# Depthwise convolution of 31 taps: four groups of taps on TensorE's column tiles in place of five, fourteen taps on VectorE in place of ten

## The chip, the cores and the metric

The kernel runs on one core of one Trainium2 chip. The metric is the device time of one execution in microseconds. The kernel before takes 2666.74 us, the median of 3 runs (2666.61 to 2668.82).

## The reference, cut to what matters

The whole program is two transformer-like blocks over 512 tokens of 1024 channels (recurrent mixers, cross attention, convolutional feed-forward stages, an expert layer). The change lies in one stage of the first block, the conformer convolution, which runs once:

```python
CONV_C = 31
def causal_dwconv(x, w, b):
    K, C = w.shape
    y = lax.conv_general_dilated(
        x, w[:, None, :], window_strides=(1,), padding=[(K - 1, 0)],
        dimension_numbers=("NWC", "WIO", "NWC"), feature_group_count=C)
    return y + b

def conformer_conv(x, norm, w1, b1, dw_w, dw_b, ln_g, ln_b, w2, b2):
    h = rms_norm(x, norm) @ w1 + b1
    h = jax.nn.glu(h, axis=-1)
    h = causal_dwconv(h, dw_w, dw_b)
    h = jax.nn.silu(layer_norm(h, ln_g, ln_b))
    return h @ w2 + b2
```

Each of the 1024 channels is convolved over time with 31 taps of its own: tap k multiplies the signal 30-k steps back.

## The kernel before, in words

Activations lie channel-major, 128 channels by 512 tokens to a tile, so the stage has 8 channel tiles, j = 0 to 7. Weights of the large products come in a stream of units of 1 MB; ScalarE rounds each (`w_hi`, L549), VectorE takes what is left (`w_lo`, L553), and a product is three matmuls, hi by hi, hi by lo, lo by hi (`split_matmul`, L566 through the helper). Three slots hold such units.

There is no scheduler. Every engine has its own program, in the order in which its function is written, and engines meet at semaphores. For the stage these are:

- **TensorE** (`pe_conformer`, L1516): first the pointwise products of tile 0; then for each j the pointwise products of tile j+1 (two banks, c1 and c2, 48 matmuls), the convolution part of tile j, and a matmul with ones over tile j-1 for the layer norm's mean. For j = 7 two key products of the next stage (`pe_keys`, of `xa_m_hi`) stand where the pointwise products would.
- **VectorE** (`dve_conformer`, L1596): for each j the gated unit `glu` into `c_t1`, then the taps one after the other, each a multiply-add of a shifted `c_t1` into `c_h` (L1649, recorded at the helper's L588), with the weights of a later tile (`c_w`, L1609) and the sum of TensorE's part of tile j-1 (`sums`, L1617) in between; then `pointwise(j+1)`: the split of a weight unit, and the two copies t2 (L1633) and t1 (L1635) out of the banks, scaled.
- **ScalarE** (`act_conformer`, L1558): the sigmoid of the gate (L1570), and tap 30 with the bias, which opens `c_h` (L1573); then the rounding of a unit. For j = 7 a rounding stands ahead of the sigmoid.
- **SyncE** (`sp_conformer`, L1499): when glu(j) is done, 16 DMAs (L1510) build four stacks of 128 partitions: 32 channels, four times over, each copy one time step later. The stacks of even j are `c_stack`; those of odd j lie in `square`, `root` and `c_mu`.

TensorE's part of the convolution: with a stack as the moving operand, one matmul with a 128 by 32 weight adds up four taps of 32 channels. Four such matmuls, one for each 32 columns of the array and 32 partitions of the bank, make a group of four taps for all 128 channels. `C_GROUPS` says how many groups there are:

```python
            for m in range(C_GROUPS):
                first = C_BASE + 4 * m
                for g in range(4):
                    mm = matmul(T, b[g * QUARTER:(g + 1) * QUARTER, first:], c_w[:, i, g * C_GROUPS + m, :],
                                c_stacks[i][g][:, 0:S - first], m == 0, m == C_GROUPS - 1)
```

and VectorE has what is left of the first 30 taps:

```python
            for k in range(CONV_C - 1 - 4 * C_GROUPS):
                s = CONV_C - 1 - k
                V.wait_ge(*dve_c.now())
                stt(V, c_h[:, j, s:], c_t1[:, i, 0:S - s], c_tap(j)(k), c_h[:, j, s:], ALU.mult, ALU.add).then_inc(
                    *dve_c.mark("tap", j, k))
```

All instructions of the stage that the steps below speak of are fp32, and each fp32 matmul has two records in the profile, so a group of four is eight records.

Of the kernel before, what the change touches and what calls it, by code (L numbers as in the profile page):

```python
# [44 lines left out]
NO_ROW = 1 << 16  # L45
LEVELS = 6
QUARTER = 32
C_GROUPS = 5

# [118 lines left out]
def _conv_taps(w):  # L170
    p = np.arange(P)
    rows = np.zeros((P, KT, 4, C_GROUPS), np.float32)
    for k in range(4):
        for m in range(C_GROUPS):
            by_tile = w[CONV_C - 2 - 4 * m - k].reshape(KT, 4, QUARTER)
# [62 lines left out]
def build(nc, stream, vectors, consts, rconsts, x_in, mem_in, gates_w, group_w, lora_w,  # L238
# [13 lines left out]
    def sb(ctx, name, shape, dt=F32):  # L252

        one = ctx.enter_context(nc.sbuf_tensor(name, shape, dt))
        over = math.prod(shape[1:]) * (1 if dt == U8 else 4) % 64
        if 0 < over <= 32:
            ctx.enter_context(nc.sbuf_tensor(f"fill{next(fill)}", [P, 8], F32))
        return one
# [65 lines left out]
    with ExitStack() as ph:  # L324
        with ExitStack() as conv:
# [3 lines left out]
            c_stack = sb(conv, "c_stack", [P, 4, S])  # L329
            c_w = sb(conv, "c_w", [P, 2, 4 * C_GROUPS, QUARTER])  # L330
            c_rows = sb(conv, "c_rows", [P, 4 * C_GROUPS * KT + QUARTER])
        with ExitStack() as inner:
# [232 lines left out]
    def matmul(T, out_ap, lhsT, rhs, first=True, last=True):  # L565
        return T.matmul(out_ap, lhsT, rhs, start=first, stop=last, skip_group_check=True)  # L566
# [949 lines left out]
    def pe_conformer(T):  # L1516
# [13 lines left out]
        for j in range(KT):  # L1530
# [7 lines left out]
            T.wait_ge(*c_stacked[j % 2].at(j, 3, 3))  # L1538
# [5 lines that stand above are left out]
# [2040 lines left out]
```

## Time and profile before

| what | value |
|---|---|
| median of 3 runs | 2666.74 us |
| profiled execution, its own time | 2666.76 us |
| its span | 2665.5 us |
| TensorE busy | 2484.3 us, 93% |
| VectorE busy | 1429.4 us, 54% |
| ScalarE busy | 925.1 us, 35% |
| granted TensorE clock, mean | 0.97 |
| the conformer's eight tiles | about 812 to 947 us of the span |

The busy shares are averages over the whole program. The change touches one stage of some 135 us, so the views of that stage are the ones to read: which engine waits there, and for whom. A row of the timeline gives start, duration, engine, line, what is written and read, the count, and in brackets the idle time before it with what ended it.

### The profile page before, as it was taken

The numbers are of one execution on the slowest core, as the hardware profiler recorded it, in microseconds if no ns is written. First come the engines' busy times: TensorE is split into PE (matmuls) and PEld (weight loads), VectorE is DVE, ScalarE is ACT, GpSimd is POOL, SyncE is SP. The second block draws the span as 40 slices with busy tenths as digits, with TensorE's granted clock in tenths as the row PEclk, the third lists the DMA queues.
The fourth block names the chain that finished last, engine by engine and source line by source line (L and its number), as shares of the span: only waits on it lengthen the run. The fifth ranks groups of instructions, "written<-read, shape, count | busy, mean of one in ns | idle before, by whom it ended". The sixth has DMA issues, their size and how long they took to land. (4 is left out here: it accounts for less than half of the span.)

```text
span 2665.5 us, 42794 instructions
## 1 busy us (share of the span) xinstructions
PE 2484.3 (93%) x18420; PEld 1867.3 (70%) x18420; DVE 1429.4 (54%) x1943; ACT 925.1 (35%) x1248; POOL 220.5 (8%) x190
## 2 busy tenths in 40 slices
PE   8989999999999989999999999998887778879997
PEld 6767877888876657878888878877666667733332
DVE  6776446454557764455454667556665746421112
ACT  4454233232333243243232344244453433411111
POOL 1002010000010000010000020001101100133331
PEclk9999999999999999999999999999898889989998
DMA  4223322322234422222222235342021134489994
GB/s 177 85 75 119 111 76 84 109 93 97 95 100 129 127 90 81 94 95 95 95 95 95 95 111 191 114 174 77 4 53 25 21 107 138 153 339 375 398 381 179
DMA packets 100570, 343.29 MB, mean 129 GB/s; under 512 B 41376, under 2 KB 49952, under 8 KB 66592
## 3 DMA queue, kind: packets, MB, share of 16 engines
q1 hardware_dynamic: 86560, 332.13, 35.4%
q0 software_dynamic: 13824, 8.44, 1.0%
q8 instruction: 147, 2.41, 0.4%
q14 instruction: 39, 0.32, 0.0%
HBM read 368.29 MB, written 30.93 MB: 150 GB/s over the span
## 5 line engine op out<-in xcount | busy, mean ns | idle before, releaser
L566 PE MATMUL bank<-xg_hi,w_hi 128*128 128x512 f32 x1504 | 597.9, 398 | 12.1 <-DVE xg_lo L588 12.1
L566 PE MATMUL bank<-xg_lo,w_hi 128*128 128x512 f32 x1504 | 586.8, 390 | 0.0
L566 PE MATMUL bank<-xg_hi,w_lo 128*128 128x512 f32 x1504 | 586.7, 390 | 0.0
L553 DVE TENSOR_TENSOR w_lo<-w_raw,w_hi 128x2048 fp32r<-128x2048 f32 x165 | 378.7, 2296 | 193.1 <-ACT w_hi L549 192.9
L549 ACT ACTIVATE w_hi<-w_raw 128x2048 fp32r<-128x2048 f32 x165 | 314.3, 1905 | 248.1 <-PE bank L566 217.8
L566 PEld LDWEIGHTS bank<-xg_hi,w_hi 128*128 128x128 f32 x1504 | 283.1, 188 | 78.4 <-DVE w_lo L553 12.3
L566 PEld LDWEIGHTS bank<-xg_lo,w_hi 128*128 128x128 f32 x1504 | 283.0, 188 | 63.9 <-issue 6.0
L566 PEld LDWEIGHTS bank<-xg_hi,w_lo 128*128 128x128 f32 x1504 | 282.9, 188 | 59.4
L566 PE MATMUL bank<-f_h_hi,w_hi 128*128 128x512 f32 x384 | 151.4, 394 | 0.0
L566 PE MATMUL bank<-f_h_hi,w_lo 128*128 128x512 f32 x384 | 150.6, 392 | 0.0
L566 PE MATMUL bank<-f_h_lo,w_hi 128*128 128x512 f32 x384 | 149.1, 388 | 0.0
L566 PE MATMUL bank<-e_over_ring,e_h_turned 128*64 128x512 f32 x560 | 124.4, 595 | 0.0
L734 DVE TENSOR_TENSOR x<-bank,x 128x512 f32<-128x512 f32 x80 | 55.0, 687 | 122.9 <-PE bank L566 122.9
L3296 DVE TENSOR_TENSOR e_he<-e_he,bank 128x256 f32<-128x256 f32 x24 | 10.1, 421 | 171.0 <-ACT e_he L3117 171.0
L588 DVE SCALAR_TENSOR_TENSOR f_g<-f_z,vec_sb,f_g 128x510 f32<-128x510 f32 x96 | 72.0, 750 | 44.2 <-ACT f_g L1445 42.5
L1445 ACT ACTIVATE f_g<-f_z,vec_sb 128x512 f32<-128x512 f32 x48 | 39.2, 816 | 150.5 <-DVE f_z L1470 150.5
L566 PEld LDWEIGHTS bank<-e_over_ring,e_h_turned 128*64 128x64 f32 x560 | 38.8, 137 | 73.0 <-issue 73.0
L566 PEld LDWEIGHTS bank<-f_h_hi,w_lo 128*128 128x128 f32 x384 | 72.1, 188 | 16.9
L566 PEld LDWEIGHTS bank<-f_h_lo,w_hi 128*128 128x128 f32 x384 | 72.1, 188 | 16.1
L566 PEld LDWEIGHTS bank<-f_h_hi,w_hi 128*128 128x128 f32 x384 | 72.3, 188 | 14.4
L662 POOL TENSOR_TENSOR square_sum<-square 128x512 f32<-128x512 f32 x7 | 10.6, 1511 | 854.1 <-ACT square L633 836.1
L627 ACT ACTIVATE xg_hi<-x,vec_sb 128x512 fp32r<-128x512 f32 x48 | 34.7, 724 | 128.8 <-DVE x L734 103.7
(493 smaller groups left out, 4278.4 us busy)
## 6 DMA issues: line engine op xcount, KB each, us to landing
w_raw<-stream SPq DMA_DIRECT2D x165, 1024.0 KB, 4.9
e_over_ring<-expert_rows SPq DMA_DIRECT2D x70, 1024.0 KB, 9.6
e_w_raw<-expert_rows SPq DMA_DIRECT2D x26, 1024.0 KB, 8.7
p_spill<-p_stage SPq DMA_DIRECT2D x36, 256.0 KB, 2.2
na_bias<-bias_na SPq DMA_DIRECT2D x32, 160.0 KB, 4.5
mix_gate<-p_spill SPq DMA_DIRECT2D x16, 256.0 KB, 3.4
e_w_raw<-y_rows SPq DMA_DIRECT2D x8, 512.0 KB, 6.7
rw_rkv<-p_spill SPq DMA_DIRECT2D x12, 256.0 KB, 5.8
```

The costliest lines, as they stand in the source:

```text
L549: A.activation(ring(m)["hi"][m % SLOTS][:, :], ring(m)["raw"][m % RAW][:, :], ACT.Copy).then_inc(*w_hi.mark(m))
L553: V.tensor_tensor(ring(m)["lo"][m % SLOTS][:, :], ring(m)["raw"][m % RAW][:, :], ring(m)["hi"][m % SLOTS][:, :].bitcast(F32), ALU.subtract ...
L566: return T.matmul(out_ap, lhsT, rhs, start=first, stop=last, skip_group_check=True)
L588: return V.scalar_tensor_tensor(out=out_ap, in0=in0, scalar=scalar, in1=in1, op0=op0, op1=op1)
L627: A.activation(xg_of(i)[0][:, j, :], x[:, j, :], ACT.Identity, scale=vcol(NORMS[i], j)).then_inc(*act_norm.mark(i, "hi", j))
L662: G.tensor_tensor(square_sum_of(i), square[:, 0, :], square[:, 1, :], ALU.add).then_inc(*pool_norm.mark(i, "sum", 1))
L734: V.tensor_tensor(x[:, j, :], held(*tag, j)[:, :], x[:, j, :], ALU.add).then_inc(*added.mark(*tag, j))
L1445: A.activation(m["g"][:, s, :], m["z"][:, s, :], ACT.Identity, scale=f_tap(l, ch)(CONV_F - 1), bias=vcol(f"f_dw_b{l}", ch)).then_inc(*act_ ...
L3296: V.tensor_tensor(e_he[:, k % 2, :], e_he[:, k % 2, :], held("e_gate", k)[:, D_EXPERT:], ALU.mult).then_inc(*dve_e.mark("he", k))
```

## The change

One constant, from which the counts of both loops, the shape of `c_w` and `c_rows`, and the array of tap weights follow:

```diff
-C_GROUPS = 5
+C_GROUPS = 4
```

`_conv_taps` lays out the weights of 4 groups (taps 29 down to 14) in place of 5 (29 down to 10); VectorE's loop runs over taps 0 to 13 in place of 0 to 9. `c_w` holds 16 blocks of 32 columns for each tile in place of 20. The number of DMAs that build the stacks is the same, 16 a tile.

On VectorE, between the taps of tile 0 and the split of the next unit (names: `c_t` is `c_t1` or `c_t2`):

```order
@@ -514,4 +514,8 @@
 L588 SCALAR_TENSOR_TENSOR c_h<-c_t,vec_sb,c_h 128x490
 L588 SCALAR_TENSOR_TENSOR c_h<-c_t,vec_sb,c_h 128x491
+L588 SCALAR_TENSOR_TENSOR c_h<-c_t,vec_sb,c_h 128x492
+L588 SCALAR_TENSOR_TENSOR c_h<-c_t,vec_sb,c_h 128x493
+L588 SCALAR_TENSOR_TENSOR c_h<-c_t,vec_sb,c_h 128x494
+L588 SCALAR_TENSOR_TENSOR c_h<-c_t,vec_sb,c_h 128x495
 L553 TENSOR_TENSOR w_lo<-w_raw,w_hi 128x2048
 L1633 TENSOR_TENSOR c_t<-bank,rstd 128x512
```

Four taps are added ahead of the split and of the copies out of the banks; the same stands in tiles 1 to 6, and in tile 7 ahead of the sum of tile 7.

On TensorE, at the end of the convolution part of tile 0 and the start of the pointwise products of tile 2:

```order
@@ -3394,5 +3394,4 @@
 L566 MATMUL bank<-c_stack,c_w 32x503 x4
 L566 MATMUL bank<-c_stack,c_w 32x499 x4
-L566 MATMUL bank<-c_stack,c_w 32x495 x4
 L566 MATMUL bank<-xg_hi,w_hi 128x512
 L566 MATMUL bank<-xg_lo,w_hi 128x512
```

The last of the five groups is gone, in every tile.

## Rows read from the trace of the kernel before

**Rows 1.** The page: span, and busy time of TensorE
```profile
span 2665.5 us, 42794 instructions
PE 2484.3 (93%) x18420; PEld 1867.3 (70%) x18420; DVE 1429.4 (54%) x1943; ACT 925.1 (35%) x1248; POOL 220.5 (8%) x190
```

**Rows 2.** Windows from t2 to t2 of a tile: length, busy us by engine, clock
```profile
843.27:859.61 16.34, 16.34 (x94) 10.51 (x90) 12.93 (x17) 3.34 (x3) 0.00 (x0) 1.00 0.46 129
...
908.61:924.94 16.33, 16.33 (x94) 10.52 (x90) 12.92 (x17) 3.38 (x4) 0.00 (x0) 1.00 0.45 129
```

**Rows 3.** Waits from 808 to 950 us: total, times, longest
```profile
DVE c_t L1633 <- PE bank L566: 11.3, 6, 2.0
...
DVE c_h L588 <- ACT c_h L1573: 7.1, 8, 0.9
...
DVE c_t L588 <- ACT c_t L1570: 3.0, 8, 1.3
```

**Rows 4.** Timeline of VectorE, one tile (j = 3) and the next t2
```profile
859.61 0.69 DVE L1633 TENSOR_TENSOR c_t<-bank,rstd 128x512 f32<-128x512 f32 x1 [1.85 <-PE bank L566]
...
861.14 0.75 DVE L588 SCALAR_TENSOR_TENSOR c_t<-c_t,vec_sb 128x512 f32<-128x512 f32 x1 [0.25 <-ACT c_t L1570]
...
868.86 3.02 DVE L588 SCALAR_TENSOR_TENSOR c_h<-c_t,vec_sb,c_h 128x488 f32<-128x488 f32 x4
871.80 2.29 DVE L553 TENSOR_TENSOR w_lo<-w_raw,w_hi 128x2048 fp32r<-128x2048 f32 x1
875.94 0.69 DVE L1633 TENSOR_TENSOR c_t<-bank,rstd 128x512 f32<-128x512 f32 x1 [1.85 <-PE bank L566]
```

**Rows 5.** The tiles c_h and c_w: count, duration min/median/max in ns, form
```profile
L588 DVE SCALAR_TENSOR_TENSOR c_h<-c_t,vec_sb,c_h x80: 720/727/732, 815.1 to 936.8; 128x482 f32<-128x482 f32 x8, 128x483 f32<-128x483 f32 x8, 128x484 f32<-128x484 f32 x8, 128x485 f32<-128x485 f32 x8
L1663 DVE TENSOR_TENSOR c_h<-c_h,c_mu x8: 683/685/693, 952.6 to 956.8; 128x512 f32<-128x512 f32 x8
L1609 DVE TENSOR_TENSOR c_w<-c_rows x8: 817/818/826, 815.8 to 913.9; 128x640 f32<-128x640 f32 x8
```

**Rows 6.** Timeline of TensorE: the convolution part of tile 0 and of tile 6
```profile
825.91 6.12 PE L566 MATMUL bank<-c_stack,c_w 128*32 128x511 f32 x40 [3.71 <-DMA c_stack<-c_t]
...
924.73 4.42 PE L566 MATMUL bank<-c_stack,c_w 128*32 128x511 f32 x40
```

**Rows 7.** Timeline of VectorE, tile 1
```profile
826.31 0.68 DVE L1633 TENSOR_TENSOR c_t<-bank,rstd 128x512 f32<-128x512 f32 x1
...
832.09 0.83 DVE L1609 TENSOR_TENSOR c_w<-c_rows 128x640 f32<-128x640 f32 x1 [0.37 <-PE bank L566]
```

**Rows 8.** Timeline of SyncE's queue, tile 7: first and last of the 16 stack DMAs
```profile
928.29 1.14 SPq L1510 DMA_DIRECT2D square<-c_t  x2
...
938.06 0.59 SPq L1510 DMA_DIRECT2D c_mu<-c_t  x1
```

**Rows 9.** Timeline around tile 7, ScalarE, VectorE and TensorE
```profile
924.90 1.91 ACT L549 ACTIVATE w_hi<-w_raw 128x2048 fp32r<-128x2048 f32 x1 [11.36 <-PE bank L566]
...
924.94 0.69 DVE L1633 TENSOR_TENSOR c_t<-bank,rstd 128x512 f32<-128x512 f32 x1 [1.85 <-PE bank L566]
...
927.51 0.75 DVE L588 SCALAR_TENSOR_TENSOR c_t<-c_t,vec_sb 128x512 f32<-128x512 f32 x1 [1.28 <-ACT c_t L1570]
...
947.36 0.69 DVE L1617 TENSOR_TENSOR c_h<-bank,c_h 128x511 f32<-128x511 f32 x1 [9.84 <-PE bank L566]
...
940.23 1.06 PE L566 MATMUL bank<-square,c_w 128*32 128x511 f32 x2 [4.37 <-DMA c_mu<-c_t]
```

**Rows 10.** Windows with the granted clock (third number from the end)
```profile
940.00:945.00 5.00, 4.77 (x24) 1.34 (x28) 0.00 (x0) 0.00 (x0) 0.00 (x0) 0.50 0.01 3
945.00:950.00 5.00, 5.00 (x38) 2.79 (x31) 1.35 (x3) 0.00 (x0) 0.00 (x0) 0.94 0.00 0
...
965.00:970.00 5.00, 2.85 (x25) 2.65 (x23) 3.43 (x5) 4.91 (x5) 0.00 (x0) 1.00 0.30 123
```

**Rows 11.** Timeline of TensorE: an idle time that the clock outlasted
```profile
970.23 0.47 PE L566 MATMUL bank<-c_s_hi,w_hi 128*128 128x512 f32 x1 [2.37 <-DVE c_s_lo L1677]
```

## The prediction, made before the changed kernel ran

> **What bounds the kernel now.** I read the page first: TensorE is busy for 93% of the span [rows 1]. That average does not price this change, since it moves work from TensorE to VectorE in one stage only. So the second view is the windows of that stage, cut from one t2 (VectorE's first copy out of a bank) to the next. A tile takes 16.33 or 16.34 us, the same in the five tiles j = 2 to 6, of which the first and the last are shown [rows 2], and TensorE is busy in all of it, VectorE in 12.9 us. TensorE sets the pace of these tiles.
>
> The third view, the waits, tells how near VectorE is behind [rows 3]. It loses 3.4 us a tile, but the kinds differ. Before t2 it waits for TensorE, 1.85 us a tile [rows 4]: that is real slack. The other waits are for ScalarE: 0.25 us for the sigmoid and 0.88 us for the tap that opens `c_h`. ScalarE starts each of those only when VectorE has handed it the operand, so they belong to VectorE's own chain and can hide nothing. The chain of one tile is thus 16.33 - 1.85 = 14.48 us; back to back, starts overlap the end before by 0.08 us, so 14.40 us from t2 to t2. The question of the change is whether its extra work fits in about 1.9 us.
>
> The stage ends on another path. glu(7) releases 16 stack DMAs that one queue issues one after another from 928.29 to 938.65 us [rows 8]; TensorE waits 4.37 us for them and starts tile 7's part at 940.23 us, and VectorE waits 9.84 us more for the sum [rows 9]. The layer norm's mean follows from that. So the end of the stage hangs on when t2(7) starts, not on VectorE's taps of tile 7.
>
> **The change part by part.**
>
> *Four more taps a tile on VectorE.* Each is 727 ns [rows 5], but a tap waits for the one before it (same `c_h`), so the pitch counts: four take 3.02 us [rows 4], (3.02 - 0.73) / 3 = 0.763 us. The new taps have 492 to 495 columns against 488 to 491 there, some 4 ns more. Four cost 4 x 0.767 = 3.07 us.
>
> The same instructions could be priced from a page. The Trainium skill, "VectorE: DVE Perf Modes", section "Side-by-side: where the cycles go for N=2048 bf16", gives one element a cycle at 0.96 GHz plus about 158 cycles of start and fill; my estimate from it is (493.5 + 158) / 0.96 = 679 ns a tap. The trace has 727 ns for the duration and 763 ns for the pitch, so the trace decides; by the page the final sum would be about 2670.6 us.
>
> *A shorter `c_w`.* It has 512 columns in place of 640. 640 take 818 ns and a two-operand instruction of 512 columns 685 ns [rows 5], so 0.13 us goes. Bounds: nothing, if the broadcast operands set the time, to 0.16 us (a fifth). I take 0.13. The net per tile is 3.07 - 0.13 = **2.93 us**, against slack of 1.9.
>
> *One group fewer on TensorE.* Five groups take 4.42 us [rows 6], so one takes 0.88. TensorE's tile falls from 16.34 to about 15.5 us. In tiles 0 to 6 this is worth nothing: VectorE's chain is now 14.40 + 2.93 = 17.33 us, and TensorE waits. Where? Not in the products: c2(j+2) ends some 14 + 15.5 = 29.5 us after t2(j) and is asked for after 2 x 17.33 = 34.7 us. It is at the start of the convolution part, because stacks(j) land 2.3 us (t2 to end of glu [rows 4]) + 11.9 us (to the start of the matmuls [rows 8, 9]) after t2(j). So the new TensorE idle time is 17.33 - 15.5 = 1.9 us a tile, ended by a stack DMA, and behind it stand the mean of tile j-1 and the products of tile j+2.
>
> *Tile by tile.* t2(1) started with no idle time ahead of it [rows 7], so tile 0 is VectorE's already: it moves by 3.07 - 2 x 0.13 = 2.80 us (two `c_w` in that tile) to 829.11. In tile 1 the 0.37 us wait of `c_w` for TensorE [rows 7] goes, since TensorE's first part ends earlier and VectorE comes later; with VectorE's 17.34 us t2(2) is at 846.45 against 843.27. Five tiles of 17.33 bring t2(7) to 933.1 against 924.94: **+8.16 us**.
>
> *Tile 7.* glu(7) waited 1.28 us for the sigmoid in place of 0.25, because ScalarE had to round a unit first, and that waited until c2(7) freed the slot at 924.9, just as t2(7) started [rows 9]. Now c2(7) ends about 5 us before t2(7), and the 1.91 us rounding is done by then: **-1.03 us**. The stacks follow glu(7) as before. Tile 7's part has a group fewer: **-0.88 us**, whatever the clock at its first groups, since the last group ran at full rate (0.94 in the window that holds it [rows 10]). The four extra taps of tile 7 (3.07 us) lie in VectorE's 9.84 us of idle time before the sum; without that cover they would be added whole.
>
> *DMAs.* The 16 stack DMAs a tile are unchanged, 10.4 us of SyncE's queue in a tile of 17.3. The tap weights' load shrinks by a sixth and lies before the stage: nothing.
>
> *The sum.* 8.16 - 1.03 - 0.88 = +6.25 us. The stages behind start later by that and are otherwise the same. The profiled execution took 2666.76 us (span 2665.5 [rows 1] and 1.3 around it), so 2673.0; the median of the runs shown is 2666.74, the same within 0.02.
>
> **The rivals.**
>
> *A. The clock falls in the new idle times.* For it: tile 0's part took 6.12 us in place of 4.42 after 3.71 us of idleness [rows 6], and tile 7's started at 0.50 of full clock, the lower level of 1.2 GHz, after 4.37 us [rows 9, 10]. Against it: after 2.37 us idle the clock stayed at 1.00 on both sides [rows 10, 11], and the new idle times are 1.9 us. The price: 5 us at half clock is 2.5 us of work, so TensorE's tile would be 15.5 + 2.5 = 18.0 us; that decides only above 17.33, and then adds 0.7 x 6 = 4 us: 2677 us. It would also use up the idle time that causes it, so not every tile would have it. [...]
>
> *B. The added taps are covered, and TensorE's gain shows (not slower).* The place is VectorE before t2. It decides if the net addition is below 1.9 us a tile. With 1.07 or less, TensorE would still pace tiles 1 to 6 at 15.5 us, and the end would be 6 x 0.88 earlier, less 0.88 for tile 7: 2666.76 - 6.2 = 2660.6 us. Whoever adds up all idle time of VectorE (16.33 - 12.92 = 3.4 us) finds room for 2.93. Against it: at least 1.13 us of that is the chain's own wait for ScalarE, and no tap is shorter than 0.72 us [rows 5].
>
> *C. The same mechanism, but smaller.* The taps pipeline better, or the stretch of low clock at tile 7's part is shorter than in the trace (5 us at 0.50 [rows 10], which cost 2.5 us): +3 to +5 us, 2670 to 2672.
>
> That the change does not do what it says is excluded by the order of its instructions shown above.
>
> **How the numbers follow.** A measurement of this kernel tells about 0.2%, 5.3 us, from no change, so the border is 2672.1, close below my forecast. The forecast case has 0.72; run to run scatter is up to 2 us (2666.61 to 2668.82), so I put 0.57 of it above the border and 0.15 below. A has 0.08, all above. C has 0.15, all within. B has 0.05, of which 0.04 faster by over 0.2%. Together: faster 0.04, same 0.31, slower 0.65. The predicted time is the forecast's, 2673.0. The range starts at 2670.0 (C, page price included) and ends at 2677.5 (A); it leaves out B and some scatter.
>
> **What would show it.** In the changed kernel's windows the pitch from t2 to t2 is 17.3 us for j = 2 to 6; VectorE's idle time before t2 is gone, the 0.25 and 0.88 us waits stay. TensorE shows six waits of about 1 to 2 us on stack DMAs (c_stack or c_mu) at the start of each part, clock at 1.00 in them. t2(7) starts near 933.1, glu(7) waits 0.25 us, tile 7's part starts near 947.4, TensorE idle about 7 us before it. From there on everything is later by 6.25 us. A pitch of 16.3 or less, or idle time left before t2, would refute the sum; a pitch near 18 with a clock below 1 means rival A; a right t2(7) and a wrong end would put the error behind the stage.

## The result, and the profile after

| | before | changed |
|---|---|---|
| median of 13 runs | 2666.74 us (2661.75 to 2674.22) | 2674.82 us (2665.30 to 2676.41) |
| ratio | | 1.0024, 95% interval 1.0016 to 1.0032 |
| profiled execution | 2666.76 us | 2676.41 us |
| span | 2665.5 us | 2675.1 us |

The change makes the kernel slower. The ratio is worked out from the single runs and not from the two medians: it stands for 6.4 us (4.3 to 8.5), while the medians are 8.1 us apart. The forecast was 6.25 us, 2673.0 in all.

The windows from t2 to t2, tiles 3 and 4 of the changed kernel (against [rows 2]):

```profile
864.37:881.69 17.32, 15.51 (x86) 10.44 (x82) 15.62 (x21) 3.35 (x3) 0.00 (x0) 1.00 0.41 122
...
881.69:899.02 17.33, 15.64 (x86) 10.44 (x82) 15.63 (x21) 3.35 (x3) 0.00 (x0) 1.00 0.42 121
```

The pitch went from 16.33 to 17.33 us. TensorE, busy all the time before, has 1.7 to 1.8 us of each of these tiles idle; VectorE's busy time rose from 12.9 to 15.6 us. Its timeline, tile 3 and the next t2 (against [rows 4]):

```profile
864.37 0.68 DVE L1633 TENSOR_TENSOR c_t<-bank,rstd 128x512 f32<-128x512 f32 x1
...
865.90 0.75 DVE L588 SCALAR_TENSOR_TENSOR c_t<-c_t,vec_sb 128x512 f32<-128x512 f32 x1 [0.25 <-ACT c_t L1570]
867.53 2.24 DVE L588 SCALAR_TENSOR_TENSOR c_h<-c_t,vec_sb,c_h 128x482 f32<-128x482 f32 x3 [0.89 <-ACT c_h L1573]
869.69 0.68 DVE L1609 TENSOR_TENSOR c_w<-c_rows 128x512 f32<-128x512 f32 x1
...
873.48 6.09 DVE L588 SCALAR_TENSOR_TENSOR c_h<-c_t,vec_sb,c_h 128x488 f32<-128x488 f32 x8
879.49 2.28 DVE L553 TENSOR_TENSOR w_lo<-w_raw,w_hi 128x2048 fp32r<-128x2048 f32 x1
881.69 0.68 DVE L1633 TENSOR_TENSOR c_t<-bank,rstd 128x512 f32<-128x512 f32 x1
```

The row of four taps (3.02 us) has become one of eight (6.09 us), `c_w` takes 0.68 in place of 0.82, and no idle time is left before t2. The two waits for ScalarE, 0.25 and 0.89 us, stand as they did: the chain carries them.

TensorE's view of the same, with the idle time before each convolution part (tiles 0, 1, 2, 3, 4, 5, 6 and 7; those of odd tiles by their first matmul):

```profile
826.53 5.29 PE L566 MATMUL bank<-c_stack,c_w 128*32 128x511 f32 x32 [3.73 <-DMA c_stack<-c_t]
...
843.56 0.62 PE L566 MATMUL bank<-square,c_w 128*32 128x511 f32 x2 [0.62 <-DMA c_mu<-c_t]
...
860.90 3.59 PE L566 MATMUL bank<-c_stack,c_w 128*32 128x511 f32 x32 [1.77 <-DMA c_stack<-c_t]
...
878.26 0.62 PE L566 MATMUL bank<-square,c_w 128*32 128x511 f32 x2 [1.81 <-DMA c_mu<-c_t]
...
895.53 3.60 PE L566 MATMUL bank<-c_stack,c_w 128*32 128x511 f32 x32 [1.69 <-DMA c_stack<-c_t]
...
913.10 1.04 PE L566 MATMUL bank<-square,c_w 128*32 128x511 f32 x2 [2.02 <-DMA c_mu<-c_t]
...
930.28 3.60 PE L566 MATMUL bank<-c_stack,c_w 128*32 128x511 f32 x32
...
948.25 1.06 PE L566 MATMUL bank<-square,c_w 128*32 128x511 f32 x2 [7.67 <-DMA c_mu<-c_t]
```

The idle times stand where they were expected, before the parts, ended by the stack DMAs; that of tile 1 is only 0.62 us. Two rows tell more. At 913.10 a first matmul takes 1.04 us in place of 0.62: after 2.02 us of idleness the clock was at its lower level. And at 930.28 there is no idle time at all: the slow part before it had pushed TensorE's work back by as much as it would otherwise have waited.

A first rounding of the next stage's norm, long behind the conformer, is at 1533.93 us before and at 1541.46 in the changed kernel, 7.5 us later; the two executions were already 0.6 us apart when the stage began. So the stage accounts for 6.95 us by its own start and end (below). The rest of the 9.65 us between the two profiled executions arises behind that point, in stages that the change does not touch, and is within the runs' scatter, 12.5 us between the fastest and the slowest run before and 11.1 us after.

### The profile page after: what moved, and what is told of

It is laid out like the page before. It is cut to its first block and busy times, and to the rows that moved or that the text cites. A ratio compares the mean times of both kernels' runs of the same rounds, so it can differ in the third digit from the quotient of the medians.

```text
span 2675.1 us, 42698 instructions
## 1 busy us (share of the span) xinstructions
PE 2480.2 (93%) x18356; PEld 1866.7 (70%) x18356; DVE 1451.2 (54%) x1975; ACT 925.7 (35%) x1248; POOL 220.5 (8%) x190
## 5 line engine op out<-in xcount | busy, mean ns | idle before, releaser
L588 DVE SCALAR_TENSOR_TENSOR c_h<-c_t,vec_sb,c_h 128x482 f32<-128x482 f32 (+6 forms) x112 | 81.5, 727 | 10.8 <-ACT c_h L1573 7.1
L566 PEld LDWEIGHTS bank<-f_h_hi,w_hi 128*128 128x128 f32 x384 | 72.2, 188 | 14.4
```

The source lines that it names most:

```text
L588: return V.scalar_tensor_tensor(out=out_ap, in0=in0, scalar=scalar, in1=in1, op0=op0, op1=op1)
```

## The experiments

For each kernel I read two things: the ratio to the kernel before, and, from its profile, the time from t2(0) to the first subtraction of the mean (L1663), which holds the whole of the eight tiles and depends on nothing behind them. Before it is 952.60 - 811.99 = 140.61 us. The ratios are to runs of the kernel before that were made beside each group of experiments (their medians: 2667.47 us for the four kernels below the change, 2667.49 for the next four, 2666.81 for the last three). They are worked out from the single runs, so they are not quotients of the medians in the table. One profiled execution stands behind each stage time, and its DMA issues alone can shift it by some tenths of a microsecond, as the point on the rest of the 0.7 us shows below.

| kernel | pitch, us | t2(0) to the mean, us | against before | median, us | ratio (95%) |
|---|---|---|---|---|---|
| before: 5 groups, 10 taps | 16.33 | 140.61 | | 2666.74 | |
| the change: 4 groups, 14 taps | 17.33 | 147.56 | +6.95 | 2674.82 | 1.0024 (1.0016 to 1.0032) |
| 4 groups, 10 taps (leaves out four taps) | 15.49 | 134.10 | -6.51 | 2661.92 | 0.9981 (0.9970 to 0.9991) |
| 5 groups, 14 taps (adds four taps twice) | 17.47 | 148.04 | +7.43 | 2676.12 | 1.0038 (1.0026 to 1.0050) |
| 6 groups, 6 taps | 17.12 | 145.78 | +5.17 | 2671.36 | 1.0016 (1.0007 to 1.0025) |
| 3 groups, 18 taps | 20.29 | 165.26 | +24.65 | 2693.63 | 1.0103 (1.0088 to 1.0118) |
| 4 groups, splits on GpSimd | 19.55 | 160.71 | +20.10 | 2688.53 | 1.0082 (1.0068 to 1.0096) |
| the same, key product early | 19.5 | 157.76 | +17.15 | 2687.64 | 1.0078 (1.0065 to 1.0092) |
| 5 groups, key product early | 16.33 | 135.15 | -5.46 | 2659.56 | 0.9974 (0.9961 to 0.9986) |
| 4 groups, key product early | 17.33 | 142.68 | +2.07 | 2670.88 | 1.0016 (1.0007 to 1.0026) |
| 5 groups, two queues | 16.33 | 128.34 | -12.27 | 2654.13 | 0.9948 (0.9934 to 0.9961) |
| 4 groups, two queues | 17.33 | 141.52 | +0.91 | 2668.11 | 0.9999 (0.9990 to 1.0008) |
| 5 groups, two queues, key early | 16.33 | 128.21 | -12.40 | 2651.73 | 0.9948 (0.9934 to 0.9961) |

### TensorE's half alone

```diff
-C_GROUPS = 5
+C_GROUPS = 4
-            for k in range(CONV_C - 1 - 4 * C_GROUPS):
+            for k in range(CONV_C - 1 - 4 * (C_GROUPS + 1)):
```

> TensorE's half of the change alone: four groups there, and VectorE keeps its ten taps. Taps 10 to 13 of the convolution are left out. If TensorE paces the kernel before and VectorE's chain alone makes the change slower, TensorE's saving now shows: pitch from t2 to t2 15.5 us in place of 16.34, VectorE idle before t2 about 1.1 us a tile, and the kernel 5 to 6.5 us faster than before (ratio 0.998). If instead the fewer matmuls themselves cost (a lower clock in a less busy TensorE), the pitch stays at 16.3 or more and the time does not fall.

The window of a tile of it, and the row of VectorE's timeline that ends the tile:

```profile
857.30:872.79 15.49, 15.49 (x86) 10.25 (x82) 12.79 (x16) 3.34 (x3) 0.00 (x0) 1.00 0.48 135
```
```profile
872.79 0.69 DVE L1633 TENSOR_TENSOR c_t<-bank,rstd 128x512 f32<-128x512 f32 x1 [1.15 <-PE bank L566]
```

As expected: TensorE is busy in all 15.49 us, VectorE waits 1.15 us for it, and the kernel is faster, by 6.5 us in the stage and 5.1 us (2.4 to 8.0) by the ratio. So the group taken from TensorE is worth 0.84 us a tile by itself, and fewer matmuls do no harm.

### VectorE's half alone

```diff
-            for k in range(CONV_C - 1 - 4 * C_GROUPS):
+            for k in range(CONV_C - 1 - 4 * (C_GROUPS - 1)):
```

> VectorE's half alone: fourteen taps there, and TensorE keeps five groups, so taps 10 to 13 are added twice. My theory: pitch 14.40 + 3.07 = 17.47 us, set by VectorE; TensorE idle about 1.1 us a tile before the convolution part; tile 7's part not shortened; 8.2 us slower than before. If the loss came from TensorE's idle time and clock, this kernel, with less idle time, would lose clearly less than the change's 6 to 8 us.

The pitch is 17.46 or 17.47 us in each of the six tiles and the loss 7.4 us by the stage, 10 us (7 to 13) by the ratio, with TensorE idle only about 1.1 us a tile (it is busy for 15.61 and 17.15 us of tiles 2 and 3). The loss does not come from TensorE's idle time: less of it, and the kernel is no faster than the change. t2(7) comes 9.24 us later than before, counted from t2(0). The stage loses 0.8 us less than the 8.2 expected, and all of that is behind t2(7): tile 7's part, expected at its old length, took 6.46 us in place of 6.99, and the part starts 1.37 us sooner after t2(7), where the sigmoid accounts for 1.04.

### Six groups, and three

The same constant, set to 6 and to 3.

> The same constant moved the other way: six groups, six taps on VectorE, nothing left out. If TensorE paces the tiles, each gets one group longer: pitch 17.2 us, VectorE idle before t2 about 5.7 us, and 5.5 to 6.5 us slower than before. If five groups were already more than the bound engine needs, the time would not change or fall.

> Three groups, eighteen taps, nothing left out. Past the knee each four taps should cost their full chain: pitch 17.33 + 2.93 = 20.27 us, t2(7) 28.6 us later than before, less 1.0 for the sigmoid and 1.7 for tile 7's part: 26 us slower than before, 2692.6 us. TensorE idle 5.6 us a tile with the clock at half at the start of each part, which stays hidden; if that clock cost something, the pitch would be above 20.5 us.

The window of a tile of six groups, that of a tile of three, and a row of VectorE's timeline with three groups:

```profile
862.00:879.14 17.14, 17.14 (x102) 10.77 (x98) 10.14 (x12) 3.35 (x3) 0.00 (x0) 1.00 0.44 127
```
```profile
874.51:894.79 20.28, 14.68 (x64) 8.34 (x62) 18.44 (x26) 3.35 (x3) 0.00 (x0) 0.83 0.35 103
```
```profile
863.21 9.18 DVE L588 SCALAR_TENSOR_TENSOR c_h<-c_t,vec_sb,c_h 128x488 f32<-128x488 f32 x12
```

The first is a tile of six groups: TensorE paces it and VectorE has 5.6 us to spare. The stage loses 5.17 us, a little under the 5.5 to 6.5 expected, and the ratio stands for 4.3 us (1.9 to 6.7). The second is a tile of three groups: VectorE paces it. Each step of four taps beyond the change costs 2.96 us a tile, as the change's own net 2.93, and the third row has twelve taps in 9.18 us, a pitch of 0.768. The clock in the three-group tile is 0.83 on average, since its part began at the lower level after 5.61 us of idleness; so did those of tiles 1 and 5, while those of tiles 2, 4 and 6, after 2.9 to 3.3 us, ran at full clock. The pitch is still VectorE's own 20.28: rival A's cause was there in half of the tiles, and cost nothing in them. By the stage the loss is 24.65 us where 26 were expected; t2(7) comes 28.74 us later (28.6 expected), and what is missing lies behind it, in a part of tile 7 that got 2.8 us shorter in place of 1.7. Five groups is the best of the four counts. The balance lies between 5 and 4, and this loop has no count between.

### The splits on GpSimd

If VectorE's chain is the cause, relieving VectorE should bring TensorE's gain out. `w_lo` of the eight units split during the stage was moved to GpSimd, which has nothing to do there, with a semaphore of its own. The second kernel also has the key product of the next experiment.

```diff
-            dve_take(V, place[("pw1", j)])
+    def pool_splits(G):
+        for m in pool_units:
+            G.wait_ge(*w_hi.at(m))
+            G.tensor_tensor(ring(m)["lo"][m % SLOTS][:, :], ring(m)["raw"][m % RAW][:, :],
+                            ring(m)["hi"][m % SLOTS][:, :].bitcast(F32), ALU.subtract).then_inc(*w_lo_pool.mark(m))
```

> The change with VectorE relieved: the eight splits w_lo of the conformer's pointwise products move from VectorE to the idle GpSimd; nothing is left out. If VectorE's chain of 17.33 us is the whole cause of the loss, the chain falls by 2.2 us to 15.1 and TensorE's 15.5 us sets the pitch again: 5.5 to 7 us faster than before (about 2661), with the same four groups and fourteen taps. GpSimd should take some 5.6 us a split (four times its 1.4 us for 512 columns), hidden. Rival: GpSimd and VectorE hinder each other on memory, the taps grow longer and the pitch stays above 16.3.

> The same, and key product 2 stands ahead of tile 7's part on TensorE instead of ahead of the last mean. It fills 3.1 us of TensorE's idle time there and leaves the way to the mean free: another 3 us if the clock still falls before tile 7's part, 5 us if it does not. 8 to 12 us faster than before, about 2657.

Both kernels were expected to be faster than the one before; by the stage they are 20 and 17 us slower. The rival holds, and more strongly than it was put. From the timeline of GpSimd and that of VectorE, the same tile:

```profile
859.15 4.85 POOL L565 TENSOR_TENSOR w_lo<-w_raw,w_hi 128x2048 fp32r<-128x2048 f32 x1 [14.69 <-ACT w_hi L555]
```
```profile
859.46 5.10 DVE L1621 TENSOR_TENSOR c_w<-c_rows 128x512 f32<-128x512 f32 x1
```

GpSimd works from 859.15 to 864.00 (4.85 us, where 5.6 were expected). VectorE's `c_w`, 0.68 us in the changed kernel, starts at 859.46 and ends at 864.56, just after GpSimd does: it got no further until GpSimd's instruction was over. So 2.2 us taken off VectorE's chain came back as 4.4 us of blocking, and the pitch is 19.55 us. By the Trainium skill ("SBUF — State Buffer", section "Who interferes with whom") a VectorE instruction with two operands in SBUF and a GpSimd instruction that reads SBUF exclude each other: the later one waits until the earlier is over. The trace agrees: 5.10 us against 0.68. The second kernel shows the same pitch; its key product gives back 3 us (157.76 against 160.71), as expected of that part. These two kernels therefore do not test what they were made for, namely whether TensorE's pace returns when VectorE is really relieved. Only the first experiment shows that, by leaving taps out; no kernel here relieves VectorE and still does all the work.

### The key product ahead of tile 7's part

```diff
-                pe_keys(T, 1, 0, 1)
+                pe_keys(T, 1, 0, 1, 2)
...
-        pe_keys(T, 1, 2)
```

> The kernel before with key product 2 ahead of tile 7's part. TensorE's idle time there falls from 4.4 to 1.3 us and the clock should stay at full level, so the part takes 4.4 in place of 7.0 us, and the last mean follows the sum of tile 7 without the 3.1 us product between: 3 to 5.5 us faster than before.

> The changed kernel with key product 2 ahead of tile 7's part. Idle time there falls from 7.7 to 4.6 us; the clock still falls; the last mean comes 2.8 us earlier: 2.8 us faster than the change, so 3.5 to 5 us slower than before. The loss of the tiles themselves (pitch 17.33) stays.

TensorE's timeline at tile 7's part and the last means, with five groups, and with four:

```profile
939.45 0.62 PE L566 MATMUL bank<-square,c_w 128*32 128x511 f32 x2 [1.41 <-DMA c_mu<-c_t]
943.80 2.00 PE L566 MATMUL bank<-c_h,const_sb 128*128 128x512 f32 x4
```
```profile
947.50 1.07 PE L566 MATMUL bank<-square,c_w 128*32 128x511 f32 x2 [4.21 <-DVE c_h L588]
952.48 2.00 PE L566 MATMUL bank<-c_h,const_sb 128*128 128x512 f32 x4
```

After 1.41 us of idleness the part runs at full clock and takes 4.35 us (6.99 before); the last two means follow in one go. The stage gets 5.46 us shorter, at the upper end of what was expected, and the kernel is faster than the one before and the changed one. With four groups the same edit gives 4.9 us (142.68 against 147.56) where I expected 2.8. The 2.8 us are there, in the way from the part to the mean (2.68 us in place of 5.48); besides, the part takes 5.0 us (947.50 to 952.48) in place of 6.4, less of it at the low clock, and the stacks come 0.7 us sooner after t2(7). The two kernels with the edit are 7.5 us apart: 8.2 us from the tiles, less 1.3 us in the way from t2(7) to the part, plus 0.6 us in the part. So the tiles' loss stays.

### Two queues for the stacks

The wait for the stacks is 16 DMAs issued one after another by SyncE's queue. Seven of them go through ScalarE's queue, after its tap 30:

```diff
-            for k in range(4):
-                for g in range(4):
-                    Y.dma_start(...)
+            stack_up(Y, j, STACK_DMAS[:9], c_stacked)
...
+            if j >= 2:
+                A.wait_ge(*pe_c.at("conv", j - 2))
+            stack_up(A, j, STACK_DMAS[9:], c_stacked_a)
```

> Five groups and ten taps as before; seven of the 16 stack DMAs of a tile go through ScalarE's queue after its tap 30, nine stay on SyncE's. Nothing is left out. Stacks should land some 4 us sooner after glu (8 in place of 12 us). TensorE's 3.7 us of idle time and half clock at tile 0's part go (5.5 us), pitch stays 16.3; tile 7's part starts 4 us sooner after t2(7) and at full clock (2.6 us): 9 to 12 us faster than before, about 2656.

> The same two queues with four groups and fourteen taps. If the loss sits in VectorE's chain, earlier stacks do not help the tiles: pitch stays 17.33 us, only tile 7's way gets 4 us shorter: 2 to 4 us slower than before. If instead the wait for the stacks were what paces the changed kernel, the pitch would fall towards 15.5 us and the time below that with five groups.

> Two queues and key product 2 ahead of tile 7's part, five groups. With the stacks early, TensorE has no idle time left there, so the order of key product and part matters little: within 1.5 us of the two queues alone, 9 to 12 us faster than before.

TensorE's part of tile 0 with five groups (timeline); then, with four, the window of a tile and TensorE's timeline at the parts of tiles 2, 3 and 7:

```profile
823.58 4.42 PE L567 MATMUL bank<-c_stack,c_w 128*32 128x511 f32 x40
```
```profile
864.77:882.11 17.34, 15.54 (x84) 10.41 (x83) 15.63 (x22) 3.46 (x3) 0.00 (x0) 1.00 0.40 122
```
```profile
856.99 3.60 PE L567 MATMUL bank<-c_stack,c_w 128*32 128x511 f32 x32 [1.71 <-DMA c_stack<-c_t]
...
874.37 0.62 PE L567 MATMUL bank<-square,c_w 128*32 128x511 f32 x2 [1.80 <-DMA square<-c_t]
...
943.71 1.07 PE L567 MATMUL bank<-square,c_w 128*32 128x511 f32 x2 [7.30 <-DMA square<-c_t]
```

With five groups everything expected comes: no idle time and full clock at tile 0 (6.12 us before [rows 6]), the pitch at 16.33 again once VectorE has taken two tiles at its own 14.4, tile 7's part without a wait; 12.3 us by the stage, and 0.9948 by the ratio, faster than both kernels and, with its sister below, the fastest here. The key product adds nothing to it that could be told, since there is no idle time left to fill: 128.21 against 128.34 us, and the same ratio. The gain has two halves: t2(7) comes 5.45 us sooner after t2(0), from the start of the tiles, and the rest, 6.8 us, lies behind t2(7).

With four groups I expected 2 to 4 us more than before and got 0.9 by the stage, and no difference by the ratio. This kernel shows what the DMA rows mean. TensorE is still released by a stack DMA and still waits 1.7 to 1.8 us, although its part starts 9.60 us after t2(3) in place of 13.89: the whole of TensorE's work has only moved earlier against VectorE's, and the pitch is 17.34 us. The row names the DMA; the cause is glu, VectorE's chain, behind it. With this improvement in both, five groups lead four by 13.2 us by the stage (141.52 - 128.34), 13.6 by the ratios: the tiles' loss, and the gain at tile 0 that VectorE's chain swallows.

## Why the prediction was right, point by point

- **The pitch.** Forecast 17.33 us (chain 14.40, plus 3.07, less 0.13); measured 17.32 to 17.33. VectorE's half alone gives 14.40 + 3.07 = 17.47, and that is what it shows. The chain itself, which the prediction only derived, can be seen bare: with two queues and five groups t2 follows t2 after 14.40 and 14.38 us in tiles 1 and 2, with no idle time ahead of t2.
- **ScalarE's waits belong to the chain.** Both stand, 0.25 and 0.89 us a tile. Rival B, which counted them as room, is refuted by the changed kernel itself and by three groups, where they stand too.
- **t2(7).** Forecast 8.16 us later; measured from t2(0) it is 933.68 - 812.59 = 121.09 against 112.95, 8.14 us.
- **TensorE's group.** Forecast 0.88 us, a fifth of 4.42; measured 0.83 to 0.84 (from the start of a part to the next mean it is 3.52 us with four groups and 4.35 with five, at full clock). So the new idle times were 1.7 to 1.8 us in tiles 2 to 4, and not 1.9. Six of 1 to 2 us were forecast: tile 1 had 0.62 us and tile 6 none.
- **The sigmoid of tile 7.** Forecast -1.03 us; t2 to glu's start is 1.53 us (2.57 before), -1.04. ScalarE's rounding was over at 932.4, before t2(7).
- **Tile 7's part.** Here the sum was off: forecast -0.88 us "whatever the clock", measured 954.67 - 948.25 = 6.42 against 6.99, -0.57. The group itself gave 0.83, but the low clock took 0.26 more than before. A group runs in two halves, its two records: seven of the eight halves ran at the low clock, against six of ten and part of a seventh before. The idle time ahead had grown from 4.37 to 7.67 us, and low clock lasted longer into a shorter part. "Whatever the clock" was the wrong premise.
- **The rest of the 0.7 us.** The stage's 6.95 us exceeds 6.25 by 0.7. Tile 7's part is 0.31 of it. The 16 DMAs of tile 7 took 0.33 us more of the queue (935.99 to 946.68, against 928.29 to 938.65), and the way from the part to the mean 0.10. The 0.33 us need not come from the change. In the profiled execution before, one issue was slow (0.95 us in place of 0.59), in that of the changed kernel a pair was (1.90 in place of 1.22), and with the key product early and four groups none was: there the series took 10.0 us.
- **The clock.** That 1.9 us of idleness leaves it alone held for four of the five new idle times (0.62 to 1.81 us), not for the one of 2.02 us. But its cost was rightly bounded: the slow part ate the next idle time, and t2 did not move. Three groups and VectorE's half each exclude rival A as the source of the loss; TensorE's half shows that fewer matmuls by themselves do no harm.
- **The size as measured.** The forecast's 6.25 us lies within the ratio's 4.3 to 8.5. The scatter was misjudged, at up to 2 us from three runs: thirteen runs of the kernel before spread over 12.5 us. Why single executions scatter so stays open; no run here was made for it. The changed kernel's median, 1.8 us above the forecast, is within that scatter; that it lies so close is in part luck, and the windows, not the median, carry the account.

## What to carry to other kernels

When work moves from the pacing engine to the second one, compare the added time with the second engine's idle time before the hand-over alone; waits that its own operands cause are part of its chain. Here 1.9 of 3.4 us were room, and 2.9 were put in. And when a stage is balanced this finely, look first at its ends: the start and the end of these eight tiles held 12 us, while taking a group from TensorE without giving VectorE anything for it brought 6.5. A wait ended by a DMA is not yet a DMA problem: ask what the DMA itself waited for.

## What the runs showed of the hardware that I had not expected

- A VectorE instruction with two SBUF operands that started 0.31 us after a GpSimd instruction of 4.85 us ended only behind it: 5.10 us in place of 0.68.
- The length of an idle time does not settle what TensorE's clock does. It fell to 1.2 GHz as the part began after 2.02 us (the change, tile 5), and it stayed at 2.4 GHz through the same part after 2.03 us in the changed kernel with the key product early, and after 3.28 us with three groups (tile 4). The granted clock in the stretch that began with the 2.02 us (third number from the end), then the two starts that ran at full rate:

```profile
913.10:916.50 3.40, 3.40 (x19) 1.06 (x23) 3.37 (x4) 0.00 (x0) 0.00 (x0) 0.51 0.02 5
```
```profile
913.02 0.62 PE L566 MATMUL bank<-square,c_w 128*32 128x511 f32 x2 [2.03 <-DMA c_mu<-c_t]
```
```profile
909.20 2.76 PE L566 MATMUL bank<-c_stack,c_w 128*32 128x511 f32 x24 [3.28 <-DVE c_h L588]
```

- A start at full rate does not mean that the clock holds. With six groups tile 7's part began at 2.4 GHz after 3.90 us of idleness, but the clock fell some 1.3 us later (granted 0.50 from 948 to 950 us), while TensorE was busy, and the part took 6.87 us in place of 5.18:

```profile
946.17 0.62 PE L566 MATMUL bank<-square,c_w 128*32 128x511 f32 x2 [3.90 <-DMA c_mu<-c_t]
```
